# Second half of three output projections as seven half-size products, tiles finished in pairs

## What is computed

```python
for layer in range(4):        # window attention, latent attention, mLSTM, window attention
    sh, sc, gt = modulation(c, w_ada, b_ada)
    h = rmsnorm(x, g_pre) * (1.0 + sc) + sh
    y = mixer(h)              # ends in  (o * silu(z)) @ w_out,  w_out is 1024 x 1024
    x = x + gt * rmsnorm(y, g_post)
```

## Time and profile before

| | us |
|---|---|
| median of 3 runs | 1606.87 (1605.59 to 1607.45) |
| the profiled execution | 1613.06 |
| its span, first to last instruction | 1611.3 |

### The profile page before, as it was taken

The page is one execution under the profiler, slowest core; times in us unless marked ns, Lnnn a source line. Parts: engine busy times, 40 slices in busy tenths (PEclk is TensorE's granted clock), DMA queues, the critical chain, the costliest instruction groups (busy, mean ns, idle before and its releaser), DMA issues.

```text
span 1611.3 us, 18886 instructions
## 1 busy us (share of the span) xinstructions
PE 1589.4 (99%) x7203; PEld 1009.2 (63%) x7203; DVE 657.0 (41%) x1605; ACT 401.4 (25%) x1058; POOL 506.1 (31%) x504
## 2 busy tenths in 40 slices
PE   8999999999999999999999999999999999999999
PEld 3874555468356448884464767558645444788854
DVE  2634344434322534763565424244522323222254
ACT  2104444321243211011452225311233320100000
POOL 1524554132153122520351316447422210010051
PEclk9999999999999999999999999999999999999999
DMA  9452230422440323224522521256533223344441
GB/s 346 185 209 106 97 157 1 163 89 75 172 177 9 130 88 123 87 97 158 208 81 105 192 104 67 73 156 163 197 114 151 105 77 132 151 143 146 146 181 68
DMA packets 23176, 210.73 MB, mean 131 GB/s; under 512 B 3160, under 2 KB 7960, under 8 KB 10672
## 3 DMA queue, kind: packets, MB, share of 16 engines
q1 hardware_dynamic: 19440, 195.74, 32.4%
q0 software_dynamic: 3648, 13.79, 3.0%
HBM read 204.75 MB, written 1.49 MB: 128 GB/s over the span
## 4 chain that ended last, share of the span: by engine, by line
PE 94%; DMA 2%; DVE 1%; POOL 1%; ACT 1%; issue 0%; SPq 0%; DVEq 0%; ACTq 0%
PE bank L739 27%; PE bank L1237 14%; PE bank L1593 9%; PE bank L883 5%; PE bank L897 5%; PE bank L1619 4%; PE bank L1532 4%; PE bank L870 3%; PE bank L1125 3%; PE bank L1115 2%; PE bank L1149 2%; PE bank L801 2%; PE bank L752 2%; PE bank L1140 1%; DMA ring<-stream 1%; PE bank L1106 1%
## 5 line engine op out<-in xcount | busy, mean ns | idle before, releaser
L739 PE MATMUL bank<-ring,arena 128*128 128x512 f32 (+2 forms) x864 | 357.1, 570 | 1.0 <-DVE arena L1679 1.0
L739 PEld LDWEIGHTS bank<-ring,arena 128*128 128x128 f32 x864 | 161.9, 190 | 176.5 <-issue 165.2
L3138 POOL TENSOR_SCALAR arena<-arena,stat 128x512 f32<-128x512 f32 (+1 forms) x128 | 168.0, 1325 | 177.0 <-DVE stat L1825 176.8
L1593 PE MATMUL bank<-arena,ring 128*128 128x256 f32 (+1 forms) x768 | 152.8, 362 | 0.0
L1593 PEld LDWEIGHTS bank<-arena,ring 128*128 128x128 f32 x768 | 136.0, 190 | 17.0 <-issue 0.5
L2715 ACT ACTIVATE arena<-arena,stat 128x513 f32<-128x513 f32 (+3 forms) x128 | 81.3, 636 | 126.1 <-DVE stat L1817 126.0
L1237 PE MATMUL bank<-arena 128*128 128x256 f32 x432 | 96.4, 379 | 0.0
L897 PE MATMUL bank<-ring,arena 128*128 128x512 f32 x192 | 89.6, 602 | 2.0 <-DMA ring<-stream 1.1
L883 PE MATMUL bank<-arena,ring 128*128 128x512 f32 (+1 forms) x256 | 90.5, 497 | 0.3 <-DVE arena L1801 0.2
L1237 PEld LDWEIGHTS bank<-arena 128*128 128x128 f32 x432 | 81.9, 190 | 11.9 <-issue 0.8
L1237 PE MATMUL bank<-arena,ring 128*128 128x256 f32 x384 | 85.4, 380 | 0.0
(11 more groups left out here) (372 smaller groups left out, 2289.6 us busy)
## 6 DMA issues: line engine op xcount, KB each, us to landing
ring<-stream SPq DMA_DIRECT2D x87, 2048.0 KB, 8.0
ring<-stream SPq DMA_DIRECT2D x6, 1024.0 KB, 9.9
arena<-arena POOLq DMA_DIRECT2D x50, 64.0 KB, 3.0
gate_rows<-gate_scratch POOLq DMA_DIRECT2D x3, 1024.0 KB, 4.8
masks_sb<-masks POOLq DMA_DIRECT2D x2, 1024.0 KB, 5.1
arena<-g_scratch POOLq DMA_DIRECT2D x1, 2048.0 KB, 10.7
arena<-rev_scratch POOLq DMA_DIRECT2D x8, 256.0 KB, 7.4
ring<-stream SPq DMA_DIRECT2D x1, 1536.0 KB, 7.2
```

Of the source, the lines that this page charges most:

```text
L739: last = mm(dst, a, b, start=(k == 0), stop=(k == len(pairs) - 1))
L1593: last = mm(ps[:, SEQ * part + cols.start:SEQ * part + cols.stop], w[:, a:a + P], hT2[:, k, cols], start=(k == 0), stop=(k == DC - 1))
L3138: nc.gpsimd.tensor_scalar(row, row, stat[:, 3, s:s + 1], None, ALU.mult).then_inc(w_norm, 1)
```

## The change

For layers 0, 1 and 2 (`SPLIT_OUT`) the second half of the output projection is no longer four products of 1024 x 512, one a tile. It is split into 2 x 2 x 2 blocks (256 tokens, 512 inputs, 256 columns), seven block products of eight matmuls 128x256 each, in banks 5, 6, 7 in turn (`split_bank`), in the order 0, 1, 2, 3, 5, 4, 6. The tokens' sums are made by VectorE in the first half, ahead of `late_sums`, which moves back by one tile each; the weights' differences by GpSimd, after the last attention output. VectorE adds the products to the four results of 256 tokens x 256 columns. Tiles 0 and 1 are complete after the fifth product, tiles 2 and 3 after the seventh. No turn stands between the products: behind the seventh come the turn of tile 0, `late_modulation`, the turn of tile 1, and the next layer, which turns tiles 2 and 3 together after its second tile (layer 3: third q product).

In the diff `split_output` is TensorE's, `split_tiles` VectorE's, `split_squares` ScalarE's, the last part GpSimd's; `add(dst, i, term, have)` adds block product i from its bank to `term`, `gate(i, n, have)` multiplies a result by the gate row into y.

```diff
+SPLIT_OUT = (0, 1, 2)
+SPLIT_ORDER = (0, 1, 2, 3, 5, 4, 6)
...
+            def split_output(layer):
+                src, slot = split_source(layer)
+                w = weights(f"{layer} out1").rearrange("p (k n) -> p k n", k=DC)
+                s1, s2, s3, s4 = split_tokens
+                t1, t2, t4 = split_weights
+                for n, i in enumerate(SPLIT_ORDER):
+                    left, right = ((part_of(src, 0, 0), part_of(w, 0, 0)), (part_of(src, 0, 1), part_of(w, 0, 1)), (s2, t2), (s1, t1),
+                                   (s3, part_of(w, 1, 0)), (s4, part_of(w, 1, 1)), (part_of(src, 1, 1), t4))[i]
+                    if i == 2:
+                        pe.wait_ge(flag("split_tokens_ready"), layer + 1)
+                        pe.wait_ge(split_sums, 4 * layer + 2)
+                    elif i == 3:
+                        pe.wait_ge(split_first, layer + 1)
+                    elif i == 5:
+                        pe.wait_ge(split_v, 7 * layer + 1)
+                    elif i == 4:
+                        pe.wait_ge(split_v, 7 * layer + 2)
+                        pe.wait_ge(split_sums, 4 * layer + 3)
+                    elif i == 6:
+                        pe.wait_ge(split_v, 7 * layer + 3)
+                        pe.wait_ge(split_sums, 4 * layer + 4)
+                    for j in range(2):
+                        for k in range(4):
+                            last = mm(split_bank(n)[:, SEQ * j:SEQ * j + SEQ], left[:, slot[k], rows(j)], right[:, k, :],
+                                      start=(k == 0), stop=(k == 3))
+                    last.then_inc(split_made, 1)
...
+                if layer in SPLIT_OUT:
+                    split_output(layer)
+                    turn_tile(f"{layer + 1} hT", 0, 4 * (layer + 1))
+                    late_modulation(layer + 1)
+                    turn_tile(f"{layer + 1} hT", 1, 4 * (layer + 1))
...
+            def split_tiles(layer):
...
+                dve.wait_ge(split_first, layer + 1)
+                add(split_outs[0][0], 1, first_part, 0)
+                gate(0, 0, 1)
+                add(part_sum, 2, first_part, 0)
+                add(other_sum, 3, part_sum, 2)
+                add(split_outs[0][1], 5, other_sum, 3)
+                gate(0, 1, 4)
+                settle()
+                add_to_x(0)
+                add_to_x(1)
+                normalise(pre, 0)
+                add(split_outs[1][1], 4, other_sum, 3)
+                add(part_sum, 4, part_sum, 2)
+                gate(1, 1, 5)
+                normalise(pre, 1)
+                add(split_outs[1][0], 6, part_sum, 6)
+                gate(1, 0, 7)
+                settle()
+                save_tile(layer + 1, 0)
+                save_modulation(layer + 1, "late")
+                add_to_x(2)
+                save_tile(layer + 1, 1)
+                add_to_x(3)
+                normalise(pre, 2)
+                normalise(pre, 3)
...
+            def split_squares(layer):
...
+                sc.wait_ge(split_made, 7 * layer + 1)
+                act_op(first_part, split_bank(0)[:, :], ACT.Copy).then_inc(split_first, 1)
+                squares_of(0, 0, 1)
+                squares_of(0, 1, 4)
+                square_pair(0)
+                squares_of(1, 1, 5)
+                save_tile(layer + 1, 0)
+                squares_of(1, 0, 7)
+                save_tile(layer + 1, 1)
+                square_pair(2)
...
+                if layer in SPLIT_OUT:
+                    split_differences(layer)
+                    for first in range(0, TILES, 2):
+                        pool.wait_ge(flag("y_squared"), y_before[layer] + TILES + 2 * first + 4)
+                        for t in range(first, first + 2):
+                            total = sq[:, 4 + 2 * t:5 + 2 * t]
+                            step(nc.gpsimd.tensor_tensor(total, total, sq[:, 5 + 2 * t:6 + 2 * t], ALU.add))
+                            step(nc.gpsimd.tensor_tensor(total, total, sq[:, 64 + t:65 + t], ALU.add))
+                            root(f"{layer} post {t}")
+                        for t in range(first, first + 2):
+                            root_of_x(f"{layer + 1} pre {t}")
```

More of the change, by code:

```diff
@@ L189, in group_stages @@
         gate = (f"{layer} gate", "v")
+        split = layer - 1 in SPLIT_OUT
         last_turn = [(f"{layer} hT", "va")]
@@ L215, in group_stages @@
             out += [(f"{layer} y0", "v" * q_tiles)]
+        if layer in SPLIT_OUT:
+            out += [(f"{layer + 1} hT", "va"), (f"{layer + 1} late", "v"), (f"{layer + 1} hT", "va")]
+            continue
         for t in range(q_tiles):
@@ L570, in build @@
             tiles = LT if layer == 3 else TILES
-            for t in range(tiles):
-                roots[f"{layer} post {t}"] = (4 + 2 * t, 5 + 2 * t, D)
-                roots[f"{NEXT[layer]} pre {t}"] = (t, t + 1, D)
+            for first in range(0, tiles, 2 if layer in SPLIT_OUT else 1):
+                pair = range(first, first + (2 if layer in SPLIT_OUT else 1))
+                for t in pair:
+                    roots[f"{layer} post {t}"] = (4 + 2 * t, 5 + 2 * t, D)
+                for t in pair:
+                    roots[f"{NEXT[layer]} pre {t}"] = (t, t + 1, D)
         for t in range(LT):
@@ L620, in y_groups, with split_bank, split_source @@
         def y_groups(layer):
-            return groups_of(f"{layer} y0") + groups_of(f"{layer} y1")
+            return groups_of(f"{layer} y0") + ([] if layer in SPLIT_OUT else groups_of(f"{layer} y1"))
+        def split_bank(n):
+            return bank[5 + n % 3]
+        def split_source(layer):
+            return (oT if KINDS[layer] == "mlstm" else qT), (SLOT_OF if KINDS[layer] == "window" else range(DC))
         assert len(branch_pairs) == BRANCH_PAIRS
@@ L1274, in output_projection @@
                 chunk = lambda k: SLOT_OF[k] if KINDS[layer] == "window" else k
-                for half in range(2):
+                for half in range(1 if layer in SPLIT_OUT else 2):
                     w = weights(f"{layer} out{half}")
@@ L2831, in mlstm @@
                 save_v(0)
-                save_tile(layer, TILES - 1)
-                for t in range(1, TILES):
+                if layer - 1 in SPLIT_OUT:
+                    save_v(1)
+                    save_tile(layer, 2)
+                    save_tile(layer, 3)
+                else:
+                    save_tile(layer, TILES - 1)
+                    save_v(1)
+                for t in range(2, TILES):
                     save_v(t)
```

130 lines of the change are left out of this document (119 added, 11 removed).

## The result

The changed kernel takes 1613.67 us (median of 5 runs, 1612.86 to 1615.88) against 1607.05 (5 runs, 1605.59 to 1607.45): a ratio of 1.0044, 95% interval 1.0029 to 1.0059. It is 6.6 us slower. I had forecast 1609.2 within 1604.5 to 1613.0, so the result lies just outside. The profiled execution spans 1614.1 us.

What follows compares the result with a forecast made beforehand. TensorE, busy 99% of the span, was taken to bound the kernel. 9.9 us of matmuls go and 12.2 us of waits come, +2.3 us: 1606.87 + 2.3 = 1609.2 us, range 1604.5 to 1613.

Steps and rivals of the forecast that it cites:

- The sum: Removed matmuls plus new waits: layer 0 0.0, layer 1 +0.4, layer 2 +1.9, together +2.3 us; chance 0.52.
- What bounds the kernel, and the products: TensorE busy 99%, so only its work counts; seven products take 24.2 us, saving 3.3 us a layer, 9.9 for three.
- VectorE ahead of the products: Token sums alternate with GpSimd's differences; first block addition at T = 12.2, 13.4, 10.8; TensorE waits 0.6 us in layer 1.
- Rival 2: VectorE late everywhere: token and late sums delay the first addition to T = 14.9 and 16.1; 1612 us; chance 0.14.
- From the fifth product to the first turn: Chain to tile 0's normalising lets the turn begin at T = 25.2; TensorE waits 1.0 us in each layer.
- From there to hT: VectorE's hT writes make the next layer's first product wait 1.0 us in layers 0 and 1; layer 3's q product 4.0.
- Tiles 2 and 3 turned together: The third product waits for ScalarE's half of tile 2's hT: 1.2 us in layer 1, 1.0 in layer 2.
- Rival 1, the clock: Wait before layer 3's first q product halves TensorE's clock, costing 2.8 us more, 1612 us; chance 0.22.
- The profiled execution as base: Profiled 1613.06 us, 0.4% above the runs' median; the difference counted the same against either, and was added to 1606.87.
- Rival 3, the chains are covered: Handovers to first turn and hT each a us shorter, only layer 3's wait stays, cut to 3; some 1601; chance 0.12.
- A loss behind the stages' ends: Sign of a wrong forecast: a stage's loss lying behind its end, in quads or attention, counted at nothing.

## Why the prediction was wrong, step by step

The bound and the price of the products were right; so were the places of the waits, but for one that did not come (layer 1) and one of 0.24 us in layer 3 that I had not counted. Two steps failed. The larger is the clock, which I had as a rival and not in the sum: 3.1 us. The smaller is the first turn, 1.44, 1.45 and 1.41 us for 1.0: 1.3 us in three layers. The sum said +2.3 and the stages say +6.8, and these two are 4.4 of the 4.5 between; the other misses cancel.

- **What bounds the kernel, and the products.** Right. Seven products take 24.3 us (311.83 - 1.44 - 286.06), for 24.2.
- **VectorE ahead of the products.** The mechanism is right, the sums alternate with GpSimd's differences:

```profile
274.90 1.39 DVE L2360 TENSOR_TENSOR arena<-arena 128x1024 f32<-128x1024 f32 x1
276.21 3.36 DVE L2361 TENSOR_TENSOR arena<-arena 128x1024 f32<-128x1024 f32 x1
...
297.45 0.68 DVE L2376 TENSOR_TENSOR arena<-probs,bank 128x512 f32<-128x512 f32 x1
...
551.96 0.68 DVE L2376 TENSOR_TENSOR arena<-probs,bank 128x512 f32<-128x512 f32 x1
```

  The first addition begins at T = 11.4 in layer 0 and 12.7 in layer 1, 0.8 and 0.7 sooner than I had it, so the 0.6 us wait of layer 1 does not exist. Rival 2 falls with it.
- **From the fifth product to the first turn: the smaller step that failed.** The update of x begins at T = 20.68, for 20.7. The failure is the next link. I wrote that nothing else of VectorE's falls into this stretch and that "the update of tile 1 stands beside the square of tile 0". In the trace it stands beside the end of the square and the root behind it, because the update of tile 0 had already held up the root of tile 1. I had asked what delays VectorE there, and not what these updates delay: small operations on GpSimd, the one behind the square 1.07 us for 0.19. I had used that very sharing for the token sums, a few lines above. The turn begins at T = 25.77 for 25.2, and TensorE waits 1.44, 1.45 and 1.41 us for 1.0. The normalising first cuts that wait to 0.57 and lengthens others, as its run shows.
- **From there to hT.** Wait 0.87 for 1.0 in layers 0 and 1. But the stretch around it is longer: a turn that a wait follows costs its whole 1.09 us, not the 0.87 by which a row is ahead of the next. I had put 0.1 us of gaps into a layer; two turns that end in a wait cost about 0.4.
- **Tiles 2 and 3 turned together.** In layer 1 a wait of 0.78 for 1.2, but the two turns took 2.17 for 1.85: 2.95 us from the end of the product, for 3.05. In layer 2 0.77 for 1.0 behind turns of 1.91. Right.
- **The sum.** Layer 0: +0.69 for 0.0. Layer 1: +0.43 for +0.4, by luck: the 0.6 that was not there paid for the 0.44 at the turn and the gaps. Layer 2: +5.7 for +1.9. The wait is 3.85 for 4.0, the q product begins at T = 34.0 for 33.4, and 3.1 of the 3.8 us that the sum lacks are the clock: 6.70 us for 3.6.
- **Rival 1, the clock: the larger step that failed.** It happened, at the price put on it (3.1 us, for 2.8; 1.8 and 2.5 in two other executions of the same wait). I gave it 0.22 although the wait was forecast at 4.0 us and the one wait of the trace with a slow product behind it was 3.82. The wait "may be 0.5 shorter" was an argument against it only if the clock holds over 3.5 us, and nothing in the trace showed that. Behind 2.65 us it held in at least five of twelve runs; with 3.85, none of 27 timed runs has a mean clock of 1.000. With the clock in the sum the forecast is 1612, and 0.44 us more at each of three first turns make it 1613.3, with layer 1's 0.6 still in it, which did not come; the runs say 1613.7.
- **The profiled execution as base.** I added the sum to the median, not to the profiled 1613.06, and that was right; but I took the 0.4% between them as noise without asking where it lay. It was the wait of the earlier trace rows and its slow clock.
- **Rival 3, the chains are covered.** Not as the kernel is written. Reordered, it is half true: layers 0 and 1 come out 1.1 and 1.3 us under the kernel before, of the 3.2 that the products save.
- **A loss behind the stages' ends.** None: between the stages the two traces run at the same distance to 0.05 us, transfers apart.

Open: why the timed runs of some kernels lie 1 to 3 us from what their stages give. The mean clocks account for a part. For the kernel with tile 1 written first, which is lower, at least five runs lack the slow product of its trace, and that trace lacks the slow clock at the kernel's start that the one before the change has. The filled ones are higher. In the traces of 24 and of 12 filling products the clock fell behind a wait for a transfer near 1180 us, in that of 14 it did not, and no filled trace shows it slow at layer 3's start. None of the six timed runs with 24 products has a mean clock of 1.000. How many of the timed runs have that other fall, and what brings it, I have not shown.

## What to carry to other kernels

Where one engine is busy all the time, a cheaper block of its work is worth what is left after the new waits. Here the products saved 9.6 us by the rows while their order spent 16.4 (11.7 of waits, 3.1 of slow clock, the rest mostly longer turns); so write down, for each wait that a change makes, what could stand there instead, before giving the change up. Beside a wait of two us or more on TensorE, or a few shorter ones close together, put the slow product that followed such waits here, in the sum and not only among the rivals. And for each small GpSimd operation on the path, ask which VectorE operation with two SBUF inputs runs at that moment: it held them up here until it ended.

## What the runs showed of the hardware

- In the traces the granted clock fell to 0.50 behind waits of 2.65, 3.25, 3.85 and 4.70 us before layer 3, with a first product of 5.4, 5.4, 5.4 to 6.7 and 5.5 us in place of 3.6: the price does not grow with the wait, and differs between executions of the same operations (6.70, 6.15, 5.41). All but the 3.25 had one or two shorter waits 4 to 6 us ahead. In the timed runs the clock held behind 2.65 in at least five of twelve and behind 3.25 in at least three of twelve.
- It also fell behind three waits of 0.57, 1.08 and 1.72 us close together. It held behind 1.44 and 0.87 us with 4 us between them, and over waits of 2.8 to 3.4 us that were filled with small products.
- Of fourteen profiled executions five waited 1.74 to 2.12 us for a transfer near 1180 us. The clock fell in three of them (1.74 with the normalising first, 2.02 with 12 filling products, 2.12 with 24) and held in two (2.08 with 14, 2.12 with the change in layer 2 alone), so the length of the wait alone does not decide it.
- A product of two 128x128 float32 operands took 0.234 us in a row of them (5.62 us for 24), two recorded instructions each; I had taken 0.13.
- GpSimd's operation on one number for each partition took 0.19 us, and 1.06 to 1.34 where it began beside a running x update of VectorE.
